# Homes and load times of the weights of three stages, and the lag of the windowed attention, in a two-block transformer kernel on one core

## The chip, the cores and the metric

The kernel runs on one core of a Trainium2 chip. The core has TensorE (PE, matrix products, with its weight loads as PEld), VectorE (DVE), ScalarE (ACT), GpSimd (POOL) and SyncE (SP, which here only issues transfers); each works through its own queue in order and waits on semaphores. The metric is the device time of one execution in microseconds, as the median of several runs.

## The reference

Two transformer blocks over 2048 tokens of width 1024, all in float32. The change touches the first block and the start of the second:

```
proj = rms_norm(x) @ w_in;  q, k, v, z_attn, u_ssm, z_ssm, g = split(proj)
attn   = windowed_gqa(q, k, v, sink, rel_table) * silu(z_attn)   # 8 heads of 64, 2 kv heads
                                                                 # blocks of 128, keys of blocks n-1, n, n+1
ssm    = ...                                                     # recurrent branch, done earlier
merged = sigmoid(g_attn) * (attn @ w_branch_attn) + sigmoid(g_ssm) * (ssm @ w_branch_ssm)
x      = x + merged @ w_out
x      = rms_norm(x) * final_gain                                # end of block one
h      = rms_norm(x) * gain * (1 + scale) + shift                # block two
proj   = h @ w_in_2   # latent q and kv, rope part, x_lru and g_lru of a recurrent branch
```

After that the second block does its recurrent branch (RG-LRU), a latent attention, an output product and a mixture of 32 experts; none of it is changed.

## The kernel before

The program is written engine by engine: `tensor`, `vector`, `scalar`, `gpsimd` and `sync` call the parts of each stage in the order in which that engine runs them. Waits name events (`at("win_ve", "O", j)` is: VectorE has finished output j); a wait for an event with a negative index is none. The on-chip memory is one array, `arena`; `reg(kb, ...)` is a place in it, kb in KB per partition, and stages reuse places by hand. A float32 product of 128 x 128 by 128 x 512 is two TensorE instructions in the trace.

**First attention (`te_win`, `ve_win`, `ac_win`, `po_win`, L1225 to L1394).** 32 jobs (16 query blocks, each in two halves of four heads). A job j has, in order: two pairs of score products (TensorE, L1233), bias and minimum (VectorE, L1248), exp with sum (ScalarE, L1259), reciprocal of the sum (VectorE, L1278), scaling of four heads by it (GpSimd, L1286, four instructions), transposes of the scaled probabilities ("turns", TensorE, L147), their evacuation by ScalarE (L152) or VectorE (L158) in alternation, products with V (TensorE, L1318), and a multiply into `attnT` (VectorE, L1335). Each engine has a loop over steps j in which it works on job j's scores and on the turns and products of job j-2; the third product and the finish belong to job j-3. Probabilities lie in four buffers `Pb`, so the reduction of job j waits for the last turn of job j-4. Jobs 0, 1, 30 and 31 have two key blocks, all others three.

**Branches (`sp_br`, `te_br`, `ve_br`).** Eight blocks d of 128 output channels, each with four tiles u of 512 tokens. A tile is four products with `attnT` into one bank and four with `ssmT` into the next; VectorE multiplies both by gates `sga`, `sgs` (1 MB each a block, loaded by SyncE, double buffered) and adds them into `mgT(d)`. The weights `BW` of a block (0.5 MB) are double buffered at 128 and 132 KB and loaded by SyncE once the whole attention is done (`win_done`) and the block two before is multiplied.

**First output (`sp_out`, `te_out`, `ve_out`, `ac_out`).** 16 row blocks i of 128 tokens, two halves c of 512 channels; a half is eight products (16 instructions). The weights `WO` (2 MB a half) lie at 128 and 144 KB and are loaded once VectorE has the last sum of the branches (`br_done`). VectorE adds x (loaded per row block by SyncE, issued behind the store of the row block before), ScalarE sums squares, VectorE norms (`rsqrt`, a chain of small operations), and norms again to `hn(i)`; TensorE transposes hn(i) in `te_out_turn` two row blocks later.

**Recurrent branch of block two (`te_ll` and others).** It starts with a product with `LX[0]` (`w_lx`, 1 MB a quarter, at 144 and 152 KB), then `te_out_turn` of row block 14, a second product, the turn of row block 15, and the latent product. Its first loads are issued by `sp_ll_first` behind the last products of the output stage.

Of the kernel before, what the change touches and what calls it, by code (L numbers as in the profile page):

```python
# [91 lines left out]
def build(nc, T, out):  # L92
    ctx = ExitStack()
    with ctx:
# [1112 lines left out]
        JOBS = 2 * NT  # L1207
# [114 lines left out]
        def sp_win(s):  # L1322
            for g in range(4):
                for n in range(80, 96):
# [4 lines left out]
                               ).then_inc(*dma(f"ld_z{g % 2}", "za", g))  # L1329

# [13 lines left out]
        def te_win(t):  # L1344
            for j in range(JOBS + 4):
                if win_jobs(j):
                    te_win_score(t, j, 0)
                if win_jobs(j - 3):
                    te_win_pv(t, j - 3, 2)
                if win_jobs(j - 2):  # L1350
                    te_win_turn(t, j - 2, 0)
                    te_win_turn(t, j - 2, 1)
                if win_jobs(j):
                    te_win_score(t, j, 1)
                if win_jobs(j - 2):
                    te_win_pv(t, j - 2, 0)
                    te_win_turn(t, j - 2, 2)
                    te_win_pv(t, j - 2, 1)

        def ve_win(v):  # L1360
            for j in range(JOBS + 4):
# [4 lines left out]
                if win_jobs(j - 2):  # L1366
                    for u in range(2):
                        if (TURN[j - 2] + u) % 2:
                            any_win_turn(v, j - 2, u)
# [3 lines left out]
                if win_jobs(j - 3):  # L1373
                    ve_win_finish(v, j - 3)
                if win_jobs(j - 2) and (TURN[j - 2] + 2) % 2:
                    any_win_turn(v, j - 2, 2)

        def ac_win(a):
            for j in range(JOBS + 4):
                if win_jobs(j):  # L1380
                    ac_win_score(a, j, 0)
                if win_jobs(j - 2):
                    for u in range(2):
                        if (TURN[j - 2] + u) % 2 == 0:
                            any_win_turn(a, j - 2, u)
# [3 lines left out]
                if win_jobs(j - 2) and (TURN[j - 2] + 2) % 2 == 0:  # L1389
                    any_win_turn(a, j - 2, 2)  # L1390
# [16 lines left out]
        BW = [reg(128, 8, 128), reg(132, 8, 128)]  # L1407
# [5 lines left out]
        def sp_br(s):  # L1413
            win_done(s)
            for d in range(8):
                i = d % 2
                s.wait_ge(*at("br_pe", "ssm", d - 2, 3))
                s.do.dma_start(BW[i].rearrange("p a b -> p (a b)"), T["w_br"][d]).then_inc(*dma(f"ld_w{i}", "w_br", d))
# [4 lines left out]
                s.do.dma_start(sgs[i], sgd[8 + d]).then_inc(*dma(f"ld_sgs{i}", "sg", d))  # L1423

# [6 lines left out]

        def te_br(t):
            win_done(t)
            for d in range(8):
                t.wait_ge(*at(f"ld_w{d % 2}", "w_br", d))
# [1690 lines left out]
```

## Time and profile before

| | |
|---|---|
| median of 3 runs | 3802.64 us (3801.28 to 3806.53) |
| the profiled execution | 3799.97 us, span 3798.2 us |
| busy share of the span | PE 93%, PEld 48%, DVE 45%, ACT 27%, POOL 26% |
| first attention | about 1247 to 1431 us |
| branches | about 1435 to 1658 us |
| first output | about 1668 to 1905 us |

Times in the profile count from the start of the span. The views used are: busy time by stretch (with the granted TensorE clock as a share of 2.4 GHz), who waited for whom, the instructions in order of time, and a line's own instructions with its transfers' time from issue to landing. In the order of time, an idle stretch before an instruction stands in brackets with what ended it, and equal neighbours are merged (xN).

### The profile page before, as it was taken

What the parts mean: (1) busy time and instruction counts of PE and PEld (TensorE: products, weight loads), DVE (VectorE), ACT (ScalarE), POOL (GpSimd) and SP (SyncE); (2) the same over time, 40 slices, a digit from 0 to 9 for tenths busy, and PEclk for the clock granted to TensorE, in tenths of its full rate; (3) what the DMA queues carried; (4) which work ended last, traced back from release to release, by engine and by line L of the source; (5) the groups of instructions that cost most, each with busy time, mean ns of one, the idle gap of its engine ahead of it and who ended that gap; (6) DMA issues with size and microseconds to landing.
All of it is one profiled execution on the core that took longest, in us unless ns stands there. A gap on an engine that the chain in (4) does not pass through costs nothing. (4 is left out here: it accounts for less than half of the span.)

```text
span 3798.2 us, 33238 instructions
## 1 busy us (share of the span) xinstructions
PE 3520.1 (93%) x11453; PEld 1840.8 (48%) x11453; DVE 1700.3 (45%) x4081; ACT 1037.5 (27%) x2543; POOL 975.9 (26%) x1362
## 2 busy tenths in 40 slices
PE   4999999999999899989999998999989987999997
PEld 3754455555445444434444445555555553444443
DVE  4656633343354672326665557534444452122121
ACT  3122222211100560002244446433322222222221
POOL 0277777200000680000000005555620001212111
PEclk7999999999999999999999999999999988999999
DMA  3134445434253002221221000001012216999997
GB/s 135 57 126 145 154 142 168 153 100 133 93 177 128 34 12 111 111 78 67 78 91 41 12 11 4 1 1 45 23 47 89 83 72 251 329 329 329 323 325 238
DMA packets 115563, 459.96 MB, mean 121 GB/s; under 512 B 13587, under 2 KB 41107, under 8 KB 103356
## 3 DMA queue, kind: packets, MB, share of 16 engines
q1 hardware_dynamic: 91484, 370.18, 27.4%
q0 software_dynamic: 18432, 67.12, 6.3%
q10 hardware_dynamic: 5472, 20.45, 1.4%
q8 instruction: 94, 1.54, 0.2%
q14 instruction: 81, 0.66, 0.1%
HBM read 340.28 MB, written 117.42 MB: 121 GB/s over the span
## 5 line engine op out<-in xcount | busy, mean ns | idle before, releaser
L142 PE MATMUL pst<-arena 128*128 128x512 f32 (+5 forms) x6938 | 2755.9, 555 | 87.6 <-DVE arena L158 34.0
L142 PEld LDWEIGHTS pst<-arena 128*128 128x128 f32 x6938 | 1301.4, 198 | 1420.5 <-issue 1264.0
L164 POOL TENSOR_TENSOR arena<-arena 128x4 f32<-128x4 f32 (+7 forms) x784 | 401.4, 512 | 463.9 <-DVE arena L2024 403.5
L164 DVE TENSOR_TENSOR arena<-arena 128x1 f32<-128x1 f32 (+8 forms) x1260 | 455.6, 362 | 95.4 <-ACT arena L2254 20.2
L147 PE MATMUL pst<-arena 128*128 128x128 f32 x2145 | 322.4, 289 | 141.6 <-DVE arena L246 52.6
L147 PEld LDWEIGHTS pst<-arena 128*128 128x128 f32 x2145 | 257.1, 147 | 299.8 <-issue 142.9
L1286 POOL TENSOR_SCALAR arena<-arena 128x384 f32<-128x384 f32 (+1 forms) x128 | 151.6, 1202 | 573.0 <-DVE arena L1278 573.0
L153 ACT ACTIVATE arena<-pst,arena 128x128 f32<-128x128 f32 (+1 forms) x630 | 244.0, 482 | 115.1 <-PE pst L147 115.1
L2201 POOL TENSOR_SCALAR arena<-arena 128x512 f32<-128x512 f32 (+3 forms) x160 | 218.3, 1383 | 174.8 <-DVE arena L164 158.6
L167 DVE TENSOR_SCALAR arena<-arena 128x1 f32<-128x1 f32 (+11 forms) x581 | 142.2, 245 | 190.1 <-DMA arena<-in_bc 78.4
L173 ACT ACTIVATE arena<-arena 128x1024 f32<-128x1024 f32 x48 | 50.7, 1057 | 628.0 <-DVE arena L1522 371.6
L2834 POOL DMA_INDIRECT out<-arena x48 | 75.9, 1581 | 492.2 <-DMA out<-arena 338.5
L170 DVE SCALAR_TENSOR_TENSOR arena<-arena,pst 128x256 f32<-128x256 f32 x96 | 43.3, 451 | 355.1 <-ACT arena L2795 353.5
L152 ACT ACTIVATE arena<-pst 128x512 f32<-128x512 f32 (+3 forms) x242 | 120.2, 517 | 253.8 <-PE pst L142 197.6
L170 DVE SCALAR_TENSOR_TENSOR arena<-arena 128x512 f32<-128x512 f32 (+4 forms) x251 | 167.0, 665 | 33.8 <-ACT arena L1735 22.1
L2248 ACT ACTIVATE arena<-pst,arena 128x512 f32<-128x512 f32 (+3 forms) x160 | 98.2, 619 | 225.2 <-DVE arena L2232 225.2
L158 DVE COPY arena<-pst 128x512 f32<-128x512 f32 (+2 forms) x202 | 108.9, 546 | 85.4 <-PE pst L147 37.8
L539 ACT ACTIVATE arena<-pst,arena 128x512 f32<-128x512 f32 x64 | 44.0, 687 | 371.5 <-PE pst L142 371.5
L2308 PE MATMUL pst<-arena 128*128 128x256 f32 (+1 forms) x576 | 142.1, 370 | 0.0
L2232 DVE TENSOR_REDUCE arena<-pst 128x2 f32<-128x1024 f32 (+2 forms) x80 | 85.3, 1066 | 126.8 <-PE pst L2216 125.7
L2795 ACT ACTIVATE arena<-pst 128x256 f32<-128x256 f32 x48 | 18.4, 384 | 442.0 <-PE pst L142 442.0
L2763 POOL DMA_INDIRECT arena<-h2d,arena x48 | 47.5, 989 | 355.6 <-DVE arena L2732 337.4
(194 smaller groups left out, 2102.9 us busy)
## 6 DMA issues: line engine op xcount, KB each, us to landing
arena<-in_w_exp SPq DMA_DIRECT2D x48, 3072.0 KB, 11.9
arena<-in_w_ada SPq DMA_DIRECT2D x48, 512.0 KB, 4.7
rotd<-arena POOLq DMA_DIRECT2D x32, 512.0 KB, 4.3
arena<-rotd SPq DMA_DIRECT2D x32, 512.0 KB, 4.8
arena<-sgd SPq DMA_DIRECT2D x16, 1024.0 KB, 7.5
arena<-pwd SPq DMA_DIRECT2D x32, 416.0 KB, 5.8
pwd<-arena SPq DMA_DIRECT2D x16, 576.0 KB, 5.8
h2d<-arena SPq DMA_DIRECT2D x17, 512.0 KB, 2.9
```

The costliest lines, as they stand in the source:

```text
L142: x = t.do.matmul(o, l, r, start=(i == 0), stop=(i == len(pairs) - 1))
L147: x = t.do.transpose(o, i, ident[0:i.shape[0], 0:i.shape[0]])
L152: return a.do.activation(o, i, ACT.Copy)
L153: return a.do.activation(o, i, ACT.Identity, bias=0.0 if bias is None else bias, scale=1.0 if scale is None else scale)
L158: return v.do.tensor_copy(o, i)
L164: own(v, s).tensor_tensor(o, a, b, op).then_inc(*inc(s, *event))
L167: own(v, s).tensor_scalar(o, a, s1, s2, o1, o2).then_inc(*inc(s, *event))
L170: own(v, s).scalar_tensor_tensor(out=o, in0=a, scalar=sc, in1=b, op0=o1, op1=o2).then_inc(*inc(s, *event))
L1286: p.do.tensor_scalar(P_x, P_x, es[:, c:c + 1], None, MUL).then_inc(*inc("win_po", *(["P", j] if x == 3 else [])))
L2201: p.do.tensor_scalar(P_x, P_x, ff[:, r % 4, x, c:c + 1], None, MUL).then_inc(*inc("mla_po", "P", n, x))
L2248: a.do.activation(ring(n, x)[:, 0:w], bank(2 * (n % 2) + x)[:, 0:w], ACT.Exp, bias=mn[:, r % 4, x, c:c + 1], scale=-1.0, accum_out=ls4[:, ...
L2308: last_ = t.do.matmul(bank(6 + x)[:, w], V2[:, 2 * hp + x, j, :], PT2[n % 4][:, 256 * l:256 * l + 256][:, w], start=(j == 0), stop=(j == 2 ...
```

## The change

Four parts:

1. In the first attention, turns and the first two products belong to job j-3 in step j, the third product and the finish to job j-4. All loops have 37 steps, not 36.
2. The weights of branch blocks 0 and 1 are loaded into new places (48 and 52 KB) during the attention, behind its last load of z; blocks 2 to 7 use 144 and 148 KB. The first two tiles of block 0 stand in TensorE's queue at the head of steps 32 and 33 of the attention, where it has no more scores. A tile waits only for the part of `attnT` that it reads.
3. The first half of w_out stays at 128 KB and is loaded once TensorE has the first product group of block 7; the second half is at 104 KB, where `ssmT` was, and is loaded at `br_done`. TensorE's first four groups go (0,0), (1,0), (0,1), (1,1) as (row block, half). The load of the final gain goes behind that of x.
4. The first two quarters of w_lx are loaded from the third row block of the output stage on, not at its end.

```diff
...
                 s.wait_ge(*at("win_ve", "O", 8 * (g - 1) - 1) if g >= 2 else at("qkv_pe", "tile", 23))
                 s.do.dma_start(Zb[g % 2], zad[:, :, g * 512:(g + 1) * 512].rearrange("m p t -> p m t")
                                ).then_inc(*dma(f"ld_z{g % 2}", "za", g))
+            for d in range(2):
+                s.do.dma_start(BW[d].rearrange("p a b -> p (a b)"), T["w_br"][d]).then_inc(*dma(f"ld_w{d}", "w_br", d))
 
         def ve_win_finish(v, j):
             n, m = j // 2, 2 * (j % 2)
...
             return 0 <= j < JOBS
 
         def te_win(t):
-            for j in range(JOBS + 4):
+            for j in range(JOBS + 5):
                 if win_jobs(j):
                     te_win_score(t, j, 0)
+                elif j < JOBS + 2:
+                    te_br_tile(t, 0, j - JOBS)
+                if win_jobs(j - 4):
+                    te_win_pv(t, j - 4, 2)
                 if win_jobs(j - 3):
-                    te_win_pv(t, j - 3, 2)
-                if win_jobs(j - 2):
-                    te_win_turn(t, j - 2, 0)
-                    te_win_turn(t, j - 2, 1)
+                    te_win_turn(t, j - 3, 0)
+                    te_win_turn(t, j - 3, 1)
                 if win_jobs(j):
                     te_win_score(t, j, 1)
-                if win_jobs(j - 2):
-                    te_win_pv(t, j - 2, 0)
-                    te_win_turn(t, j - 2, 2)
-                    te_win_pv(t, j - 2, 1)
+                if win_jobs(j - 3):
+                    te_win_pv(t, j - 3, 0)
+                    te_win_turn(t, j - 3, 2)
+                    te_win_pv(t, j - 3, 1)
 
         def ve_win(v):
-            for j in range(JOBS + 4):
+            for j in range(JOBS + 5):
...
                 if win_jobs(j - 1):
                     ve_win_sum(v, j - 1)
-                if win_jobs(j - 2):
+                if win_jobs(j - 3):
...
-                if win_jobs(j - 3):
-                    ve_win_finish(v, j - 3)
+                if win_jobs(j - 4):
+                    ve_win_finish(v, j - 4)
...
         def po_win_all(p):
             for j in range(JOBS):
...
         sga = [reg(160, S), reg(176, S)]
         sgs = [reg(168, S), reg(184, S)]
         m1, m2 = reg(152, 512), reg(154, 512)
-        BW = [reg(128, 8, 128), reg(132, 8, 128)]
+        BW = [reg(48, 8, 128), reg(52, 8, 128)] + 3 * [reg(144, 8, 128), reg(148, 8, 128)]
 
         def gate_stored(e, d):
             for n in range(4 * d, 4 * d + 4):
...
             win_done(s)
             for d in range(8):
                 i = d % 2
-                s.wait_ge(*at("br_pe", "ssm", d - 2, 3))
-                s.do.dma_start(BW[i].rearrange("p a b -> p (a b)"), T["w_br"][d]).then_inc(*dma(f"ld_w{i}", "w_br", d))
+                if d >= 2:
+                    if d >= 4:
+                        s.wait_ge(*at("br_pe", "ssm", d - 2, 3))
+                    s.do.dma_start(BW[d].rearrange("p a b -> p (a b)"), T["w_br"][d]
+                                   ).then_inc(*dma(f"ld_w{i}", "w_br", d))
                 s.wait_ge(*at("br_ve", "sum", d - 2, 3))
                 gate_stored(s, d)
                 s.do.dma_start(sga[i], sgd[d]).then_inc(*dma(f"ld_sga{i}", "sg", d))
                 gate_stored(s, 8 + d)
                 s.do.dma_start(sgs[i], sgd[8 + d]).then_inc(*dma(f"ld_sgs{i}", "sg", d))
+            s.wait_ge(*at("br_pe", "attn", 7, 0))
+            s.do.dma_start(WO[0].rearrange("p a b -> p (a b)"), T["w_out"][0]).then_inc(*dma("ld_w0", "w_out", 0))
 
         def br_bank_free(b):
             if b < 4:
...
                 return PT_evac(TURN[JOBS] - 2 + (b - TURN[JOBS]) % 2)
             return at("win_ve", "O", JOBS - 2 + b - 6)
 
+        def te_br_tile(t, d, u):
+            us = slice(u * 512, (u + 1) * 512)
+            t.wait_ge(*at(f"ld_w{d % 2}", "w_br", d))
+            for j in range(8 * u + 6, 8 * u + 8):
+                t.wait_ge(*at("win_ve", "O", j))
+            t.wait_ge(*(at("br_ve", "m1", d - 1, u) if d else br_bank_free(2 * u)))
+            mm(t, bank(2 * u), [(BW[d][:, k, :], attnT[:, k, us]) for k in range(4)]
+               ).then_inc(*inc("br_pe", "attn", d, u))
+            t.wait_ge(*(at("br_ve", "m2", d - 1, u) if d else br_bank_free(2 * u + 1)))
+            mm(t, bank(2 * u + 1), [(BW[d][:, 4 + k, :], ssmT[k][:, us]) for k in range(4)]
+               ).then_inc(*inc("br_pe", "ssm", d, u))
+
         def te_br(t):
-            win_done(t)
             for d in range(8):
-                t.wait_ge(*at(f"ld_w{d % 2}", "w_br", d))
-                for u in range(4):
-                    us = slice(u * 512, (u + 1) * 512)
-                    t.wait_ge(*(at("br_ve", "m1", d - 1, u) if d else br_bank_free(2 * u)))
-                    mm(t, bank(2 * u), [(BW[d % 2][:, k, :], attnT[:, k, us]) for k in range(4)]
-                       ).then_inc(*inc("br_pe", "attn", d, u))
-                    t.wait_ge(*(at("br_ve", "m2", d - 1, u) if d else br_bank_free(2 * u + 1)))
-                    mm(t, bank(2 * u + 1), [(BW[d % 2][:, 4 + k, :], ssmT[k][:, us]) for k in range(4)]
-                       ).then_inc(*inc("br_pe", "ssm", d, u))
+                for u in range(0 if d else 2, 4):
+                    te_br_tile(t, d, u)
 
         def ve_br(v):
             win_done(v)
...
         hn = [reg(180 + 4 * i, 1024) for i in range(2)]
         junk4 = reg(188, 1024)
         ss2, rin2 = cols[:, 144:160], cols[:, 160:176]
-        WO = [reg(128, 8, 512), reg(144, 8, 512)]
+        WO = [reg(128, 8, 512), reg(104, 8, 512)]
 
         def h1_evac(i, hb):
             return at("out_ac" if hb else "out_ve", "h1", i, hb)
 
         def sp_out(s):
             br_done(s)
-            s.do.dma_start(fgb, T["fgb"]).then_inc(*dma("ld_fgb", "fgb"))
-            for c in range(2):
-                s.do.dma_start(WO[c].rearrange("p a b -> p (a b)"), T["w_out"][c]).then_inc(*dma(f"ld_w{c}", "w_out"))
+            s.do.dma_start(WO[1].rearrange("p a b -> p (a b)"), T["w_out"][1]).then_inc(*dma("ld_w1", "w_out", 1))
             for i in range(NT + 1):
                 if i < NT:
                     s.wait_ge(*at("out_ve", "x1", i - 2, 1))
                     s.do.dma_start(xt[i % 2], T["x"][i * 128:(i + 1) * 128, :]).then_inc(*dma(f"ld_xt{i % 2}", "x", i))
+                    if i == 0:
+                        s.do.dma_start(fgb, T["fgb"]).then_inc(*dma("ld_fgb", "fgb"))
+                    if i == 2:
+                        sp_ll_weights(s)
                     if i == NT - 1:
                         sp_ll_first(s)
                     s.wait_ge(*at("out_ve", "x2", i))
...
             br_done(t)
             for i in range(NT):
                 for c in range(2):
-                    b = (2 * i + c) % 4
-                    t.wait_ge(*at(f"ld_w{c}", "w_out"))
-                    t.wait_ge(*at("out_ve", "x1", i - 2, c))
-                    mm(t, bank(b), [(mgT(k)[:, i * 128:(i + 1) * 128], WO[c][:, k, :]) for k in range(8)]
-                       ).then_inc(*inc("out_pe", "x1", i, c))
+                    i_, c_ = (c, i) if i < 2 else (i, c)
+                    t.wait_ge(*at(f"ld_w{c_}", "w_out", c_))
+                    t.wait_ge(*at("out_ve", "x1", i_ - 2, c_))
+                    mm(t, bank((2 * i_ + c_) % 4),
+                       [(mgT(k)[:, i_ * 128:(i_ + 1) * 128], WO[c_][:, k, :]) for k in range(8)]
+                       ).then_inc(*inc("out_pe", "x1", i_, c_))
                 if i >= 2:
                     te_out_turn(t, i - 2)
 
...
             s.do.dma_start(lp[:, :, 0:8], T["lrup"]).then_inc(*dma("ld_lrp", "lrup"))
             for c in range(2):
                 s.wait_ge(*at("out_pe", "x1", NT - 1, c))
-            s.do.dma_start(LX[0].rearrange("p a b -> p (a b)"), T["w_lx"][0]).then_inc(*dma("ld_w0", "w_lx", 0))
             s.do.dma_start(WL.rearrange("p a b -> p (a b)"), T["w_lat"]).then_inc(*dma("ld_lat", "w_lat"))
             s.do.dma_start(pI, T["posb"]).then_inc(*dma("ld_pos", "pos"))
-            s.do.dma_start(LX[1].rearrange("p a b -> p (a b)"), T["w_lx"][1]).then_inc(*dma("ld_w1", "w_lx", 1))
+
+        def sp_ll_weights(s):
+            for i in range(2):
+                s.wait_ge(*at(f"ld_w{i}", "w_out", i))
+                s.do.dma_start(LX[i].rearrange("p a b -> p (a b)"), T["w_lx"][i]).then_inc(*dma(f"ld_w{i}", "w_lx", i))
 
         def sp_ll(s):
             s.wait_ge(*at("out_pe", "h1", NT - 1, 1))
```

`ac_win` changes its indices in the same way.

## Rows read from the trace of the kernel before

**Rows 1.** Busy time by stretch: stretch, us, each engine's busy us, PEclk, DMA, GB/s

```profile
1256.00:1258.00 2.00, 2.00 (x9) 1.55 (x9) 0.51 (x1) 0.60 (x1) 2.00 (x3) 0.50 0.00 0
...
1320.00:1360.00 40.00, 35.89 (x226) 17.34 (x228) 28.93 (x96) 24.86 (x76) 35.30 (x29) 1.00 0.08 27
...
1445.00:1660.00 215.00, 211.80 (x494) 93.48 (x492) 64.81 (x94) 0.00 (x0) 0.00 (x0) 1.00 0.20 74
```

**Rows 2.** Waits of TensorE, 1240 to 1435: total us, times, longest

```profile
PE pst L147 <- POOL arena L1286: 19.9, 17, 3.3
```

**Rows 3.** Order of time, TensorE, steady attention: start, us, what

```profile
1322.47 0.92 PE L1233 MATMUL pst<-arena 64*128 64x384 f32 x4
...
1324.96 1.09 PE L147 MATMUL pst<-arena 128*128 128x128 f32 x8 [0.99 <-POOL arena L1286]
...
1330.13 1.09 PE L147 MATMUL pst<-arena 128*128 128x128 f32 x8
...
1334.60 0.65 PE L1318 MATMUL pst<-arena 128*64 128x256 f32 x4
...
1336.24 1.09 PE L147 MATMUL pst<-arena 128*128 128x128 f32 x8 [0.99 <-POOL arena L1286]
```

**Rows 4.** GpSimd: two jobs in the order of time; its line L1286, ns min/median/max

```profile
1263.63 9.77 POOL L1286 TENSOR_SCALAR arena<-arena 128x384 f32<-128x384 f32 x8 [4.61 <-DVE arena L1278]
...
L1286 POOL TENSOR_SCALAR arena<-arena x128: 912/1242/1247, 1251.8 to 1427.3; 128x384 f32<-128x384 f32 x112, 128x256 f32<-128x256 f32 x16
```

**Rows 5.** Order of time, ScalarE, the last exp of a step in steady attention

```profile
1325.22 0.18 ACT L1259 ACTIVATION_READ_ACCUMULATOR arena<-arena 128x1 f32 x1
```

**Rows 6.** Order of time, GpSimd, its first two jobs

```profile
1251.79 7.24 POOL L1286 TENSOR_SCALAR arena<-arena 128x256 f32<-128x256 f32 x8 [548.23 <-DVE arena L1278]
```

**Rows 7.** Order of time, end of the attention and start of the branches

```profile
1415.17 1.09 PE L147 MATMUL pst<-arena 128*128 128x128 f32 x8 [1.12 <-POOL arena L1286]
...
1424.65 1.09 PE L147 MATMUL pst<-arena 128*128 128x128 f32 x8
1425.35 0.60 ACT L152 ACTIVATE arena<-pst 128x512 f32<-128x512 f32 x1 [1.80 <-PE pst L147]
...
1425.99 1.19 PE L1318 MATMUL pst<-arena 128*64 128x256 f32 x8 [0.25 <-ACT arena L152]
...
1435.16 15.21 PE L142 MATMUL pst<-arena 128*128 128x512 f32 x31 [4.36 <-DMA arena<-in_w_br]
```

**Rows 8.** Line L1423, loads of `sgs` (behind those of `sga`): landing

```profile
DMA to landing us min/median/max: 7.4/8.0/13.3
```

**Rows 9.** VectorE's last sum, TensorE's first products of w_out, landing of L1481

```profile
1657.56 0.69 DVE L164 TENSOR_TENSOR arena<-arena 128x512 f32<-128x512 f32 x1
...
1667.83 42.83 PE L142 MATMUL pst<-arena 128*128 128x512 f32 x96 [11.03 <-DMA arena<-in_w_out]
...
DMA to landing us min/median/max: 9.0/12.1/15.1
```

**Rows 10.** Order of time, VectorE, first two row blocks of the output stage

```profile
1683.22 0.69 DVE L1522 TENSOR_TENSOR arena<-pst,arena 128x512 f32<-128x512 f32 x1 [6.08 <-PE pst L142]
...
1694.30 0.69 DVE L1522 TENSOR_TENSOR arena<-pst,arena 128x512 f32<-128x512 f32 x1 [4.86 <-DMA arena<-in_x]
...
1696.96 0.69 DVE L1522 TENSOR_TENSOR arena<-pst,arena 128x512 f32<-128x512 f32 x1 [1.96 <-PE pst L142]
...
1705.94 0.75 DVE L167 TENSOR_SCALAR arena<-arena 128x1024 f32<-128x1024 f32 x1
```

**Rows 11.** Order of time, TensorE and hn(14) of VectorE, end of the output stage

```profile
1905.59 8.83 PE L142 MATMUL pst<-arena 128*128 128x512 f32 x16 [4.14 <-DMA arena<-in_w_lx]
...
1909.76 0.75 DVE L167 TENSOR_SCALAR arena<-arena 128x1024 f32<-128x1024 f32 x1
...
1922.00 1.04 PE L147 MATMUL pst<-arena 128*128 128x128 f32 x8
...
1931.13 30.29 PE L142 MATMUL pst<-arena 128*128 128x512 f32 x72 [2.08 <-DVE arena L170]
```

More of the change, by code:

```diff
@@ L1365, in ve_win @@
                     ve_win_sum(v, j - 1)
-                if win_jobs(j - 2):
+                if win_jobs(j - 3):
                     for u in range(2):
-                        if (TURN[j - 2] + u) % 2:
-                            any_win_turn(v, j - 2, u)
+                        if (TURN[j - 3] + u) % 2:
+                            any_win_turn(v, j - 3, u)
                 if win_jobs(j):
@@ L1372, in ve_win @@
                     ve_win_sink(v, j)
-                if win_jobs(j - 3):
-                    ve_win_finish(v, j - 3)
-                if win_jobs(j - 2) and (TURN[j - 2] + 2) % 2:
-                    any_win_turn(v, j - 2, 2)
+                if win_jobs(j - 4):
+                    ve_win_finish(v, j - 4)
+                if win_jobs(j - 3) and (TURN[j - 3] + 2) % 2:
+                    any_win_turn(v, j - 3, 2)
         def ac_win(a):
-            for j in range(JOBS + 4):
+            for j in range(JOBS + 5):
                 if win_jobs(j):
                     ac_win_score(a, j, 0)
-                if win_jobs(j - 2):
+                if win_jobs(j - 3):
                     for u in range(2):
-                        if (TURN[j - 2] + u) % 2 == 0:
-                            any_win_turn(a, j - 2, u)
+                        if (TURN[j - 3] + u) % 2 == 0:
+                            any_win_turn(a, j - 3, u)
                 if win_jobs(j):
@@ L1388, in ac_win @@
                     ac_win_sink(a, j)
-                if win_jobs(j - 2) and (TURN[j - 2] + 2) % 2 == 0:
-                    any_win_turn(a, j - 2, 2)
+                if win_jobs(j - 3) and (TURN[j - 3] + 2) % 2 == 0:
+                    any_win_turn(a, j - 3, 2)
         def po_win_all(p):
```

## The prediction

> **What bounds the kernel now.** I read the stages that the diff touches, in three steps. First the table by stretch: between 1320 and 1360 us (first attention) TensorE is busy 35.9 of 40 us, in the branches (1445 on) 211.8 us for 494 instructions, that is 0.429 us each and no hole until 1656.8 [rows 1]. So in these stages TensorE's own queue sets the end, and a hole in it costs its full length. Then who made the holes: in the first attention and its run-in, GpSimd's scaling of the probabilities ended 19.9 us of TensorE's waits, 17 of them, the longest 3.3 [rows 2]. Last the joints between the stages, where it waits for weights: 4.36 us for w_br [rows 7], 11.03 us for w_out [rows 9], 4.14 us for w_lx [rows 11]. The change is aimed at these four places. Everything later keeps its order and only starts earlier.
>
> **1. Three steps of lag in the steady attention.** One job now goes from turns to turns in 5.17 us (1324.96 to 1330.13), the next in 6.11 (to 1336.24), 11.28 a pair, and the wait stands in the second: its last product starts at 1334.60 and lasts 0.58, so the job was through at 1335.18 and waited 1.06 [rows 3]. GpSimd isn't full: two jobs in a row take it 9.77 us, 4.885 a job [rows 4], against 5.64 on average. It starts late, since its reciprocal comes from VectorE one step later; a third step gives its result 5 us more. Then the floor is TensorE. The job that waits for nothing takes 5.05 (1330.13 to 1335.18). For its neighbour, whose first turn is evacuated by ScalarE, the wait has so far hidden something: ScalarE's exps of that step end at 1325.40, 2.9 us after the score's start at 1322.47; a copy and its signal take 0.64 (1425.35 to 1425.99), so the first product can't start before 3.5 to 3.55, where TensorE would be there after 3.30 [rows 3, 5, 7]. I take 0.2 for it: 5.25, and 10.3 a pair, 5.15 a job. Bounds: 5.05 (no new wait) and 5.64 (nothing won).
>
> Four probability buffers remain. Job j's score reduction waits for the last turn of job j-4, which TensorE now issues one step earlier, ahead of the score itself; so no new wait of VectorE, and nothing is queued behind one. The three queues are re-ordered alike, no instruction is added.
>
> **The run-in.** GpSimd starts at 1251.79, does two jobs with two keys in 7.24, to 1259.03, then 4.885 each [rows 4, 6]. So job 3 is ready at 1268.80, and TensorE, held at job 2 until 1263.97, turns it at about 1269.1. From there 5.15 a job, less 0.6 for shorter scores at the end: turns of job 28 at 1269.1 + 25 x 5.15 - 0.6 = 1397.2, now 1415.17 [rows 7]. Gain 18.0. The 3.3 us hole before the first turns (at 1255.5), after which the clock stood at 0.50 [rows 1, 2], gets 1.7 us of scores and splits into pieces; if the clock falls all the same, job 3 is turned 1.5 later (low end of the gain).
>
> **2. First two branch tiles inside the run-out.** A tile is 8 products of two instructions, 16 x 0.429 = 6.86 us [rows 1]. From the turns of job 28: rest of that step 3.4, tile 6.86, job 29 3.7, tile 6.86, third product of 29 0.6, job 30 2.53, job 31 2.53 (1424.65 to 1427.18 now), 26.5 in all: the attention ends at 1423.7 with two tiles done. GpSimd's last job is through some 6.5 us after the last score, covered by the first tile; the turns of jobs 29 and 30 stand behind the tiles in TensorE's queue, and with them only work of this same run-out. Today the first tile starts at 1435.16 after a hole of 4.36, and its first instructions run slow: 31 take 15.21 us, not 13.3 [rows 7]. Its weights are loaded from about 1351 on, in the middle of the attention, 80 us ahead, so their price is nothing. Thirty tiles remain, 205.8 us: the branches end at 1629.5 against 1656.8. **Gain of parts 1 and 2: 27.3 us.**
>
> The cover for the gates: SyncE still issues them only after the last output of the attention, and VectorE needs both for the first tile. The second of the two landed after 7.4 to 13.3 us [rows 8]; TensorE now has two tiles, 13.7 us, before it wants the first bank back, and 17.2 before the second. With the median (8.0) that leaves some 8 us; with the longest (13.3, plus 0.7 for the multiply) it still holds. Cost 0, upper bound 2. The wait for landed w_br stands in TensorE's queue at the first tile, long met. Weights of block 2 are issued behind the gates of block 1 and needed 41 us later. Moving weights behind the gate loads at d = 3 costs nothing for the same reason.
>
> **3. w_out.** The first half now has a home that no branch weight uses and is issued when TensorE begins block 7, some 25 us ahead; both halves need 15.1 us today [rows 9]. So TensorE waits only for VectorE's last sum, which ends at 1658.25, 1.45 after the branches' last product [rows 1, 9]: a hole of 1.5 in place of 11.03. The slow start goes too: 96 instructions took 42.83, not 41.2 [rows 9]; the hole of 2.08 in [rows 11] was followed by none. The second half is issued at the sum, as the first transfer, 2 MB. The first half, with 0.5 MB ahead, landed 9.0 us after its issue [rows 9]; TensorE wants the second at 13.7 thanks to the order (0,0), (1,0), (0,1), (1,1). Covered by 4 us.
>
> But that order has a price. Row block 0 is complete at S+20.6 (S the start of the stage) where it was at +13.7, and VectorE's chain hangs on it: from the add of (0,1) to the add of (1,0), through norm, store and the load of x that SyncE issues only behind them, 11.08 us (1683.22 to 1694.30); from (1,1) to the end of hn(0) 9.7 (1696.96 to 1706.69) [rows 10]. So hn(0) ends at 20.7 + 11.1 + 0.7 + 9.7 = S+42.2, and TensorE wants it at S+41.2. A new wait of 1.0 us, once. Branch end to turn(0) is 1.5 + 42.2 = 43.7, now 1710.5 - 1656.8 = 53.7 (its 96 instructions, 42.8 less the overlap of their modelled end, behind 1667.83) [rows 9]. **Gain 10.0 us.** SyncE's new wait (first product of block 7) has only the w_out load and the next stage behind it. The two loads of w_lx now go out behind the third x, done 10 us before SyncE's next.
>
> **4. w_lx.** Gone are the 4.14 us and the slow first instructions (16 in 8.83, not 6.9) [rows 11], 6.0 together. What is late next is hn(14), which VectorE ends at 1910.51; TensorE would be there 6.86 after 1901.4, at 1908.3, so 2.2 comes back, and from turn(15) to the first gates (9.13 us, 1922.00 to 1931.13, with the existing wait of 2.08) nothing moves [rows 11]. Turn(15) then comes at 1910.6 + 0.9 + 6.9 = 1918.4, 3.6 earlier than 1922.0. **Gain 3.6 us.** Bounds 2 and 6.
>
> **Sum:** 27.3 + 10.0 + 3.6 = 40.9 us. The profiled execution took 3799.97 (span 3798.2), so 3759.1; the median of the runs stands 2.7 above it: 3802.64 - 40.9 = **3761.7 us**.
>
> **Clock.** The rows show the low level (0.50, 1.2 GHz) after holes of 3.3 us and more, full clock behind the one of 2.08 [rows 11], and full clock through the 1 us holes of the attention [rows 1 to 3]. All holes I expect are below 2.5.
>
> **A rule against lag.** The row first: GpSimd's instructions on three keys have a median of 1242 and a maximum of 1247 ns, though VectorE's sum and difference of each job fall into them [rows 4]. The Trainium skill (SBUF — State Buffer, section "SBUF: two separate sides") says that GpSimd and VectorE share one port pair under an exclusive lock, and that a VectorE operation with two SBUF inputs blocks GpSimd for its whole length. By it GpSimd, with 95% of the new step taken, would be stretched. The trace shows no stretching.
>
> **Rivals.**
> - **GpSimd becomes the bound** (0.06). If two or three small VectorE operations a job (0.17 us each) held it, a job would last 5.4: 25 x 0.25 = 6 us less, **3768**. For: 4.885 leaves only 0.26. Against: the maximum of 1247 ns. It is the lock rule's result.
> - **The lag wins nothing** (0.06), because another loop (ScalarE's exps, evacuation, product) holds the job near 5.6: 25 x 0.45 = 11 less, **3773**. Against: the free job of 5.05.
> - **New joint waits or low clock** (0.12): gates at their longest landing 2, low clock at run-in 1.5 and after the 1.5 us hole 1.5, third joint only 2: 5 to 7 less, **3767**.
> - **A bit more** (0.13): 5.05 a job and full 6 at w_lx: 5 more, **3757**.
> - **Slower than before** (0.02): the four-buffer ring. If VectorE's reduction of job j had to follow the last turns of j-4 in series, each step would be 5.15 + 1.2 (two reductions) + 0.6 (exp) = 6.95, 1.3 over today's for 32 steps, +42, against 9 + 10 + 3.6 from the run-out and the joints: **3822**. It decides from 6.35 a job on. Against: that turn stands before the score in TensorE's own queue.
> - **The change doesn't do what it says** (0.01): loads still late because SyncE is stuck in an earlier wait, **3775**. Its waits there are all for things long past.
> - My forecast, 3761.7 within 3: 0.60.
>
> **How the numbers follow.** 3755 to 3772 takes in the forecast, the better case, the joint case and the lock; it leaves out the useless lag, the ring and the last, 0.09, and what I have missed, some 0.1. About 0.2% (8 us) is what a measurement can tell; all cases but the ring and something unforeseen lie further below than that: faster 0.95, same 0.02, slower 0.03.
>
> **What would show it.** Right: turns every 5.1 to 5.3 us without waits for GpSimd after job 3; no wait for w_br, w_out or w_lx; the attention with two tiles over near 1424; holes of 1.5 before the first product of w_out, 1 before turn(0), 2.3 before turn(14). Wrong: waits of TensorE's products for ScalarE's copies over 0.3 each; GpSimd instructions beyond 1250 ns; clock below 1 behind a 1.5 us hole; the first multiply of the branches later than 13 us after the last attention output.

## The result, and the profile after

| | before | after |
|---|---|---|
| median | 3801.96 us (3799.89 to 3806.53, 4 runs) | 3764.33 us (3749.46 to 3767.74, 4 runs) |
| ratio after to before | | 0.9885, 95% interval 0.9857 to 0.9912 |
| the profiled execution | 3799.97 us, span 3798.2 | 3749.46 us, span 3747.6 |

The median moved 37.6 us, the profiled execution 50.5. When two numbers for one change differ like this, the first thing to do is to cut both spans at the same two events: TensorE's first score product of the attention, and the first gate products of the recurrent branch of block two (at 1931.13 before [rows 11]). Busy time by stretch of the kernel before, cut there (stretch, its length, busy us of the five engines, PEclk, DMA share, GB/s):

```profile
0.00:1247.74 1247.74, 1168.79 (x3418) 632.62 (x3419) 588.71 (x1046) 247.09 (x429) 412.74 (x843) 0.98 0.39 130
1247.74:1931.13 683.39, 638.61 (x2192) 296.72 (x2193) 351.29 (x1144) 170.50 (x465) 151.96 (x129) 0.98 0.22 79
1931.13:3798.20 1867.07, 1712.69 (x5843) 911.50 (x5843) 760.29 (x1892) 619.92 (x1649) 411.22 (x390) 0.96 0.38 130
```

and of the kernel after:

```profile
0.00:1234.14 1234.14, 1166.17 (x3418) 632.07 (x3419) 581.55 (x1046) 247.25 (x429) 424.14 (x843) 0.98 0.40 132
1234.14:1880.43 646.29, 632.79 (x2192) 294.46 (x2193) 351.28 (x1144) 168.89 (x465) 151.99 (x129) 1.00 0.23 84
1880.43:3747.60 1867.17, 1714.65 (x5843) 911.87 (x5843) 759.84 (x1892) 620.92 (x1649) 412.22 (x390) 0.96 0.38 130
```

The changed stages took 37.1 us less (683.39 to 646.29), and TensorE was idle 44.8 us in them before (683.39 less 638.61), 13.5 after; the other 5.8 us of the gain are busy time, products that no longer run at the lower clock (PEclk 0.98 and 1.00). The last stretch is the same to 0.1. The other 13.6 us lie ahead of the first score, where the code is unchanged; they are no gain of the change (more on this below). From here on every time of a stage is counted from the first score, which makes executions comparable to a few tenths as far as the joints. There the slow starts (the first products behind a long hole, run at the lower clock) differ between executions of one kernel: two executions of the kernel before differ by 3.2 us at the first gates, three of the kernel after by 2.0.

**Attention.** TensorE in the order of time, after, three turns in a row, then GpSimd over four jobs, its line L1286 (ns min/median/max), and all that TensorE waited for between 1240 and 1435:

```profile
1318.54 1.09 PE L147 MATMUL pst<-arena 128*128 128x128 f32 x8
...
1323.59 1.09 PE L147 MATMUL pst<-arena 128*128 128x128 f32 x8
...
1328.80 1.09 PE L147 MATMUL pst<-arena 128*128 128x128 f32 x8
```

```profile
1309.55 9.96 POOL L1286 TENSOR_SCALAR arena<-arena 128x384 f32<-128x384 f32 x8 [0.31 <-DVE arena L1278]
1319.81 9.96 POOL L1286 TENSOR_SCALAR arena<-arena 128x384 f32<-128x384 f32 x8 [0.30 <-DVE arena L1278]
```

```profile
L1286 POOL TENSOR_SCALAR arena<-arena x128: 914/1248/1278, 1238.2 to 1392.3; 128x384 f32<-128x384 f32 x112, 128x256 f32<-128x256 f32 x16
```

```profile
PE pst L1318 <- ACT arena L152: 2.4, 5, 0.7
PE pst L147 <- POOL arena L1286: 0.8, 1, 0.8
PE pst L1233 <- DVE arena L1248: 0.4, 1, 0.4
PE pst L1318 <- DVE arena L158: 0.3, 1, 0.3
```

Steps of 5.05 and 5.21 in place of 5.17 and 6.11 [rows 3], and one wait for GpSimd, 0.8, in place of 17 with 19.9 [rows 2]. A row of eight of GpSimd's instructions is two jobs with the short pause between them counted in, so its busy time is read from the view by stretch, 18 jobs before and 12 after (the fifth engine is GpSimd):

```profile
1286.18:1387.67 101.49, 92.14 (x578) 44.44 (x580) 73.80 (x244) 62.76 (x190) 88.22 (x73) 1.00 0.06 22
```

```profile
1309.55:1371.14 61.59, 61.01 (x386) 29.64 (x386) 48.88 (x163) 41.15 (x127) 58.93 (x49) 1.00 0.10 35
```

GpSimd works 4.90 us a job before and 4.91 after, now in a step of 5.13: it is nearly full (58.93 of 61.59) and no slower. Single instructions last up to 1278 ns, 1247 before [rows 4].

**Run-out and start of the branches**, TensorE:

```profile
1388.14 7.13 PE L142 MATMUL pst<-arena 128*128 128x512 f32 x16
...
1398.98 7.13 PE L142 MATMUL pst<-arena 128*128 128x512 f32 x16
...
1409.09 1.09 PE L147 MATMUL pst<-arena 128*128 128x128 f32 x8
1410.43 1.19 PE L1318 MATMUL pst<-arena 128*64 128x256 f32 x8 [0.25 <-ACT arena L152]
1411.55 38.89 PE L142 MATMUL pst<-arena 128*128 128x512 f32 x90
```

The two tiles stand between the last jobs, the third tile follows the last attention product with no hole, and 90 instructions run in 38.89 us, full clock from the first one (31 took 15.21 in [rows 7]). VectorE's first two multiplies wait for their gates, and nobody waits for them:

```profile
1416.97 0.69 DVE L164 TENSOR_TENSOR arena<-pst,arena 128x512 f32<-128x512 f32 x1 [4.88 <-DMA arena<-sgd]
1419.43 0.69 DVE L1468 TENSOR_TENSOR arena<-pst,arena 128x512 f32<-128x512 f32 x1 [1.77 <-DMA arena<-sgd]
```

**The later joints**, TensorE: first products of w_out, turn(0), turn(14), the second product of w_lx, first gates (turn(i) is the transpose of hn(i)), then the stretch behind turn(14)'s start:

```profile
1619.32 41.47 PE L142 MATMUL pst<-arena 128*128 128x512 f32 x96 [1.51 <-DVE arena L164]
1661.70 1.09 PE L147 MATMUL pst<-arena 128*128 128x128 f32 x8 [0.91 <-DVE arena L167]
...
1861.82 1.93 PE L147 MATMUL pst<-arena 128*128 128x128 f32 x8 [2.24 <-DVE arena L167]
1863.54 7.92 PE L142 MATMUL pst<-arena 128*128 128x512 f32 x16
...
1880.43 30.28 PE L142 MATMUL pst<-arena 128*128 128x512 f32 x72 [2.08 <-DVE arena L170]
```

```profile
1861.82:1865.20 3.38, 3.38 (x10) 2.40 (x11) 2.02 (x9) 1.41 (x4) 0.00 (x0) 0.51 0.13 50
```

1.51 in place of 11.03 [rows 9], the new wait of 0.91 for hn(0), and 2.24 for hn(14) in place of 4.14 for w_lx [rows 11]. One thing is new: the turn behind the 2.24 us hole took 1.93, not 1.09, and the product after it 7.92, not 7.03. The clock fell: 0.51 was granted in these 3.4 us.

### The profile page after: what moved, and what is told of

Same layout as the page of the kernel before. It is cut to its first block and busy times, and to the rows that moved or that the text cites. A ratio compares the mean times of both kernels' runs of the same rounds, so it can differ in the third digit from the quotient of the medians.

```text
span 3747.6 us, 33237 instructions
## 1 busy us (share of the span) xinstructions
PE 3513.6 (94%) x11453; PEld 1838.4 (49%) x11453; DVE 1692.7 (45%) x4081; ACT 1037.1 (28%) x2543; POOL 988.4 (26%) x1362
## 5 line engine op out<-in xcount | busy, mean ns | idle before, releaser
L164 POOL TENSOR_TENSOR arena<-arena 128x4 f32<-128x4 f32 (+7 forms) x784 | 412.7, 526 | 465.3 <-DVE arena L2043 404.9
L164 DVE TENSOR_TENSOR arena<-arena 128x1 f32<-128x1 f32 (+8 forms) x1260 | 445.4, 354 | 95.3 <-ACT arena L2273 20.2
L1286 POOL TENSOR_SCALAR arena<-arena 128x384 f32<-128x384 f32 (+1 forms) x128 | 151.7, 1213 | 523.8 <-DVE arena L1278 522.6
```

What stands on the lines that cost most here:

```text
L164: own(v, s).tensor_tensor(o, a, b, op).then_inc(*inc(s, *event))
L1286: p.do.tensor_scalar(P_x, P_x, es[:, c:c + 1], None, MUL).then_inc(*inc("win_po", *(["P", j] if x == 3 else [])))
```

## The experiments

All numbers in us from the first score, each from one profiled execution: the first turns of job 28, the end of the branches, the turns of row blocks 0 and 13 in the output stage, and the first gate products of block two. The branches end 1.51 ahead of the first product of w_out (in kernels that wait for weights there, by that hole). How sure one number is can be seen from kernels that are alike up to it: seven executions with the attention and branches of after end the branches at 383.6 to 383.7, the two of before at 409.1 and 409.6.

| kernel | turns job 28 | branches end | turn(0) | turn(13) | first gates |
|---|---|---|---|---|---|
| before | 167.4 | 409.1 | 462.8 | 652.7 | 683.4 |
| before_again | 167.6 | 409.6 | 464.9 | 654.8 | 686.6 |
| lag_alone | 150.5 | 391.4 | 445.2 | 635.1 | 666.6 |
| weights_alone | 167.7 | 403.3 | 447.2 | 637.2 | 666.0 |
| lag_undone | 167.6 | 401.6 | 445.1 | 635.1 | 662.2 |
| tiles_late_b | 150.5 | 384.1 | 427.6 | 617.6 | 644.7 |
| order_undone | 150.6 | 383.7 | 427.7 | 617.7 | 644.7 |
| wout_late | 150.6 | 383.7 | 437.7 | 627.7 | 654.7 |
| lx_late | 150.6 | 383.7 | 427.3 | 617.3 | 648.7 |
| after | 150.6 | 383.7 | 427.6 | 617.5 | 646.3 |
| after_again | 150.6 | 383.7 | 427.3 | 617.2 | 644.3 |
| after_third | 150.6 | 383.7 | 427.7 | 617.6 | 644.7 |
| joints | 150.5 | 383.6 | 426.5 | 616.4 | 641.5 |

**1. lag_alone**: the kernel before with the lag and nothing else.

```diff
...
                 if win_jobs(j - 3):
-                    te_win_pv(t, j - 3, 2)
-                if win_jobs(j - 2):
-                    te_win_turn(t, j - 2, 0)
-                    te_win_turn(t, j - 2, 1)
+                    te_win_turn(t, j - 3, 0)
+                    te_win_turn(t, j - 3, 1)
...
```

> The kernel before with three steps of lag and nothing else. My theory (GpSimd's result came one step late, TensorE is the floor): turns 5.05 and 5.21 us apart as in the kernel after, turns of job 28 at 150.6 us from the first score (167.4 before), the last product of the branches at 389 us from the first score (409.1 before), since the run-out no longer waits for GpSimd but still stands before late weights; 20 us less in all, about 3782. Rival, that GpSimd's rate or the port pair it shares is the bound: 5.4 or more a job, 8 us less at most. Rival, that the gain came from the run-in with its low clock: steps stay 5.17 and 6.11, 5 us less.

Measured: steps of 5.05 and 5.22, turns of job 28 at 150.5, as in after. Both rivals fall: the steps changed, so it was not the run-in alone, though that gave part of it (job 3 is turned at 22.4 in place of 26.0, 3.6 of the 16.9 us at job 28). Ratio to before 0.9969 (0.9946 to 0.9991), medians 3788.01 and 3807.08. Branches end at 391.4, not 389. About half of the miss is that the attention ends 18.9 us earlier, not 20; the other half is that the joint behind grew by 1.2:

```profile
1410.55 1.18 PE L1318 MATMUL pst<-arena 128*64 128x256 f32 x8 [0.25 <-ACT arena L152]
1416.30 8.92 PE L142 MATMUL pst<-arena 128*128 128x512 f32 x14 [4.57 <-DMA arena<-in_w_br]
```

The wait for weights is 4.57 here, 4.36 in [rows 7], and 14 instructions take 8.92 where 6.3 is full speed (14 x 0.429, and 0.27 more for the modelled end of a row's last product): a slow start of 2.6, against 1.6 in [rows 7], where 31 take 15.21 and full speed is 13.6. Work that is saved ahead of such a joint does not shorten it. Gain of the lag alone at the branches' end: 17.7.

**2. lag_undone**: after with two steps of lag.

> The kernel after with two steps of lag again; early weights, the two branch tiles in the run-out and the later loads stay. My theory: steps 5.17 and 6.11 as before, turns of job 29 at 172.3 us from the first score, and then the tiles hide GpSimd's last two jobs, so the branches end at 401 us from the first score (383.7 in the kernel after), 17 to 18 us more than after, though the lag alone gives 20: the two parts share the last 2 us. If they did not overlap it would be 403.5. About 3782.

Measured: branches end at 401.6, 17.9 more than after, ratio 0.9942 (0.9917 to 0.9967). The place was right (401), the overlap was not: the lag is worth 17.9 on top of the rest and 17.7 alone, so the parts seem to add up. Two effects of some 1.2 us cancel: the tiles are worth 1.7 at two steps of lag (the turns of the last two jobs stand behind tiles here with no wait) and 0.4 at three, and lag_alone paid 1.2 more at its joint. With neither in play, from weights_alone to tiles_late_b below, the lag is worth 19.2.

**3. tiles_late_b**: after with the first two tiles behind the attention.

```diff
-                elif j < JOBS + 2:
-                    te_br_tile(t, 0, j - JOBS)
...
-                for u in range(0 if d else 2, 4):
+                for u in range(4):
```

(and SyncE waits for the first product of blocks 0 and 1 before it loads blocks 2 and 3.)

> The kernel after with the first two tiles of the branches back at the head of the branch stage; weights still loaded early, with a wait of SyncE before it loads those of blocks 2 and 3. Theory A, mine: once the weights lie ready and the lag hides GpSimd, the run-out has no hole worth a tile; TensorE waits only some 0.5 us for the last output and the clock does not fall: branches end at 383 to 384 us from the first score, as in the kernel after (383.7). Theory B: the tiles are what covers the last jobs and the gate loads; without them TensorE waits some 5 us and starts slow, branches end at 389 or later.

```profile
1408.71 1.19 PE L1318 MATMUL pst<-arena 128*64 128x256 f32 x8 [0.25 <-ACT arena L152]
1409.83 20.44 PE L142 MATMUL pst<-arena 128*128 128x512 f32 x47
```

TensorE's first tile follows the last product at once, with no hole and no slow start; the tile needs only the outputs of the first eight jobs. Branches end at 384.1, 0.4 later than in after. Theory A holds, and the hole is even smaller than the 0.5 I gave it. Whole time: ratio 0.9927 (0.9900 to 0.9954), medians 3768.98 and 3807.08, six runs from 3756.8 to 3781.3: far too coarse for a difference of 0.4.

**4. weights_alone**: the same with two steps of lag as well.

> The kernel after with two steps of lag and the first two branch tiles behind the attention: of the first two parts of the change only the early weights are left. Mine: the attention ends as before, 183.5 us from the first score, TensorE waits only for the last output, some 0.5 us, and nothing starts slow; branches end at 403.5 us from the first score (409.1 before, 401.6 with the tiles at the same lag, 383.7 in after). So tiles are worth 2 us where GpSimd is waited for and 0.4 where not. Rival, that a wait for gates stands behind: 405 or more.

```profile
1429.33 1.09 PE L147 MATMUL pst<-arena 128*128 128x128 f32 x8 [1.09 <-POOL arena L1286]
...
1431.79 18.72 PE L142 MATMUL pst<-arena 128*128 128x512 f32 x43
```

Branches end at 403.3 (403.5 expected). Against lag_undone the tiles are worth 1.7, about what TensorE waits in this run-out (1.09 for GpSimd's last job, shown, and 0.54 for a copy of VectorE), and with three steps of lag 0.4. The early weights are worth 409.1 - 403.3 = 5.8: hole and slow start.

**5. order_undone**: the kernel after with the first four groups of w_out in plain order.

```diff
-                    i_, c_ = (c, i) if i < 2 else (i, c)
+                    i_, c_ = i, c
```

> The kernel after with the first four groups of the output product in plain order (0,0), (0,1), (1,0), (1,1). Mine: the second half of w_out lands 7.5 to 8 us after the stage's start, TensorE wants it at 6.9, a hole of about 1 there; the hole of 0.9 before the first turn goes, since row block 0 is complete 6 us earlier; first turn at 42.0 us from the stage's start, 42.4 in the kernel after: no difference. Rival, that the order is what hides the load: hole of 3 us or more and a slow start, first turn at 45 or later.

```profile
1627.25 7.13 PE L142 MATMUL pst<-arena 128*128 128x512 f32 x16 [1.51 <-DVE arena L164]
1635.34 34.60 PE L142 MATMUL pst<-arena 128*128 128x512 f32 x80 [0.96 <-DMA arena<-in_w_out]
1669.78 1.04 PE L147 MATMUL pst<-arena 128*128 128x128 f32 x8
```

The hole is 0.96 at the second group and none at turn(0), which comes 42.5 after the stage's start (42.0 expected, 42.4 in after). The order trades one hole of a microsecond for another. It decides nothing here.

**6. wout_late**: after with both halves of w_out loaded at the branches' end.

> The kernel after with both halves of w_out loaded at the end of the branches. Mine: the first half lands some 7.6 us after its issue, so a hole of 9.2 us and a slow start of 1.5; the second half is hidden by the order of the groups; from the last branch product to turn(0) 53 us, not 43.9: 9 more. Rival, that the new order of the groups alone recovers most of it: 48 or less.

```profile
1639.35 43.87 PE L142 MATMUL pst<-arena 128*128 128x512 f32 x96 [9.49 <-DMA arena<-in_w_out]
1683.88 1.09 PE L147 MATMUL pst<-arena 128*128 128x128 f32 x8 [0.66 <-DVE arena L167]
```

A hole of 9.49 and 2.4 of slow start (43.87 against 41.47 in after); from the branches' end to turn(0) 54.0 us, 43.9 in after. The early load is worth 10.1.

**7. lx_late**: after with the loads of w_lx behind the last output product.

```diff
-                    if i == 2:
-                        sp_ll_weights(s)
...
+            sp_ll_weights(s)
             s.do.dma_start(WL.rearrange("p a b -> p (a b)"), T["w_lat"]).then_inc(*dma("ld_lat", "w_lat"))
```

> The kernel after with the first two loads of w_lx issued behind the last output products, as before. Mine: TensorE waits 4.1 us for them and starts slow, the hole ahead of turn(14) goes, and from turn(13) to the first gates 30.7 us pass instead of 27.0. Rival, that a chain through VectorE sets this joint: 28 or less.

```profile
1872.95 9.59 PE L142 MATMUL pst<-arena 128*128 128x512 f32 x16 [4.13 <-DMA arena<-in_w_lx]
1882.38 1.04 PE L147 MATMUL pst<-arena 128*128 128x128 f32 x8
```

From turn(13) to the first gates 31.5 us (30.7 expected). The hole of 4.13 comes back, the one ahead of turn(14) goes, as expected; the start is slower than in [rows 11] (9.59 for 16 instructions, 8.83 there). The early load is worth 4.4 against after_again.

**8. after_again and after_third**: the kernel after twice more.

> The kernel after once more, for its spread and the clock behind the hole of 2.24 us ahead of turn(14). Mine: within the changed stages nothing moves (branches end 383.7 us from the first score, turn(0) 42.4 after the output stage's start); the whole time moves by some 10 us between executions with a stage ahead of the change (its first score lies anywhere from 1232 to 1248 us); the clock behind that hole stays at full speed this time as in three other kernels with the same hole, and from turn(13) to the first gates 27.0 us pass, not 28.8. Rival: the clock falls there every time in this kernel.

> The kernel after once more beside it. Mine: 39 us less than before in the changed stages (first gates 644.3 us from the first score, or 646 where the clock falls behind the hole of 2.24 us), and 39 give or take 6 in the whole time, the rest of the 48 that the last comparison showed being chance. Rival, that the change also shortens the stretches around it: 45 or more again.

Behind the same hole as in after, the clock stayed up (after_again):

```profile
1875.54 1.09 PE L147 MATMUL pst<-arena 128*128 128x128 f32 x8 [2.24 <-DVE arena L167]
1876.47 7.03 PE L142 MATMUL pst<-arena 128*128 128x512 f32 x16
```

and turn(13) to first gates took 27.1 in both, not 28.8. Whole times: 3763.60 against 3811.31, ratio 0.9873 (0.9854 to 0.9893), and 3769.99 against 3806.24, ratio 0.9901 (0.9878 to 0.9924). The first ratio stands for 48 us, the second for 38, which is what the stages say; and their intervals overlap; so nothing shows that the extra 10 of the first belong to the change.

**9. before_again**: the kernel before against itself.

> The kernel before, unchanged, against itself: what a comparison of whole times can tell here. Mine: a ratio within 0.3% of 1, stages of the change as known (branches end 409.1 us from the first score, first gates 683.4); the stretches ahead of the first score and behind the first gates differ by up to 15 us between executions. Rival, that this execution's stretches ahead and behind are the same as in the first profile (1247.7 and 1867.1).

Ratio 1.0000 (0.9986 to 1.0015), with single runs from 3794.18 to 3810.74. I had expected the stages to come as before; they are 3.2 us longer than in the first profile (686.6): the joints again, with a hole of 5.03 for w_br and slower starts at w_out and w_lx. The stretch ahead took 1250.4, the one behind 1868.4. Counted against this execution, the change is worth 42.3 and 41.9 us in the two repeats of after, not 39.1 and 38.7.

**10. joints**: after with x of the second row block loaded at the stage's start, both first products of w_lx ahead of turns 14 and 15, and hn(15) ahead of the evacuation of turn 14.

```diff
...
                 if n < LJ:
                     te_ll_project(t, n, 0)
-                if n == 0:
-                    te_out_turn(t, NT - 2)
...
                 if n < LJ:
                     te_ll_project(t, n, 1)
                 if n == 0:
+                    te_out_turn(t, NT - 2)
                     te_out_turn(t, NT - 1)
...
```

> The kernel after with three edits at the joints: SyncE loads x for the second row block at the stage's start, not behind the first store; TensorE does both products of the first w_lx block ahead of turns 14 and 15; VectorE forms hn(15) before it evacuates turn 14. Mine: the hole ahead of turn(0) goes (first turn 41.2 us from the stage's start, 42.4 in after), the one ahead of turn(14) goes, turn(13) to the first gates takes 25.5 us, not 27.0, since a wait of some 3 us for the first convolution stays; 2 to 3 us less than after in these stages, too little to tell in the whole time. Rival: the chain behind turn(15) only moves, so gates come no earlier than with 27.0.

```profile
1863.57 1.91 PE L147 MATMUL pst<-arena 128*128 128x128 f32 x16
1865.72 6.25 PE L142 MATMUL pst<-arena 128*128 128x448 f32 x16 [0.24 <-DVE arena L161]
1874.10 31.98 PE L142 MATMUL pst<-arena 128*128 128x512 f32 x72 [2.12 <-DVE arena L170]
```

Turn(0) 41.3 after the stage's start with no hole, turn(13) to gates 25.1 (25.5 expected): 2.8 less than after_again at the gates. But here the clock fell behind the hole of 2.12 at the gates (72 instructions in 31.98, 30.28 in after), which gave 1.7 back. Median 3757.62 (5 runs), ratio to before 0.9861 (0.9842 to 0.9881); beside after_again's 0.9873 on the same chip the whole time can't tell it apart.

## Why the prediction was right, point by point

The forecast was 3761.7, measured 3764.3, within the range. In the stages 40.9 us were forecast and 37.1 measured in the profiled execution, 39.1 and 38.7 in the two repeats against the same before, 42.3 and 41.9 against before_again: the forecast lies inside what two executions of either kernel leave open.

- **Lag.** 5.15 a job forecast, (5.05 + 5.21)/2 = 5.13 measured. The mechanism (a result one step late, TensorE the floor) stands by lag_alone. Turns of job 28 came at 150.6 where the sum says 149.5. The miss is in the run-in: job 3 is turned at 22.4, not at 21.4, since three products ahead of it wait 0.56 to 0.68 each for ScalarE's copies, which stand behind its exps; one of them:

```profile
1248.87 1.08 PE L1318 MATMUL pst<-arena 128*64 128x256 f32 x8 [0.68 <-ACT arena L152]
```

  I had charged that wait to the steady step only, where it costs 0.16. The clock, at 0.50 in the run-in of before [rows 1], stayed at 1.00 in that of after, whose longest hole is 0.79; the 1.5 us that I held ready for a fall were not needed.
- **The lock rule.** I wrote that the trace shows no stretching and gave the rival 0.06. Single instructions of GpSimd did pass 1250 ns, which I had set as a sign against me: up to 1278 in after, 1284 in after_again. But in lag_alone and joints, with the same steps, medians are 1242 and 1241 and maxima 1263 and 1258, and a job takes 4.90 in before and lag_alone (58.82 for 12) and 4.91 in after. So the shorter step brought no stretching that costs anything, and the longer instructions differ by execution. The Trainium skill (SBUF — State Buffer, "SBUF: two separate sides") names VectorE's operations with two SBUF inputs as what holds the port; no run here takes them out, so what they cost GpSimd is not shown. GpSimd stays 0.2 under TensorE's step, and it would be the bound next.
- **Tiles in the run-out.** 26.5 forecast for the run-out with two tiles, 26.85 measured (1384.70 to 1411.55; a tile between other products takes 7.07, not 6.86); the rest of the branches 206.3, not 205.8. Together with the run-in: 25.4 for parts 1 and 2, not 27.3. Undone one after the other, the parts are the lag 19.2 (weights_alone less tiles_late_b), the early weights 5.8 (before less weights_alone) and the tiles 0.4 (tiles_late_b less after). So what failed in the reasoning is the credit: once the weights lie ready and the lag hides GpSimd, the run-out has nothing left for the tiles to cover.
- **Slow starts.** The sum read them 0.27 too long each, as it compared a row, whose last product carries a modelled end, with 0.429 an instruction: 1.6 at the branches, not 1.9, 1.4 at w_out (42.83 less 41.47), not 1.6. They are also no constant of the joint: before_again has 1.4, 2.9 and 2.8 at the three joints.
- **Gates.** VectorE had them some 5 and 7 us after the last output, and they cost TensorE nothing, as said.
- **w_out.** 43.7 forecast from the branches' end to turn(0), 43.9 measured; hole 1.5 and 1.51; wait for hn(0) 1.0 and 0.91. wout_late gives the early load 10.1. The second half landed 7.9 us after its issue, wanted at 13.7; but the order that bought this slack won nothing (order_undone), since its price of 0.9 at hn(0) is what it saves.
- **w_lx.** 3.6 forecast, 2.0 measured in the profiled execution, 3.6 in the repeats (30.7 less 27.1). The term was right and the clock was the miss: I had taken all holes below 2.5 us as harmless, from one of 2.08 with full clock behind it.
- **Whole time.** That it came so near the median has luck in it: the four runs of after spread by 18 us on their own, and in the profiled one all three terms fell short, by 1.9, 0.2 and 1.6 us.

Open: what makes the stretch ahead of the attention 1232 to 1252 us long. The profiles show where. TensorE's holes there, before:

```profile
376.89 3.52 PE L628 MATMUL pst<-arena 128*16 128x128 f32 x16 [5.31 <-DVE arena L164]
...
453.03 0.69 PE L147 MATMUL pst<-arena 128*128 128x128 f32 x2 [6.71 <-DMA arena<-pwd]
```

and after:

```profile
441.19 0.41 PE L147 MATMUL pst<-arena 128*128 128x128 f32 x2 [1.76 <-DVE arena L164]
```

The executions with the short stretch (after, lag_undone, joints: 1232 to 1234 us) have only the small hole, the others both large ones or their like (order_undone, in between at 1242, only the second), after_again and after_third with the same code as after among them. So it isn't the change. Why VectorE's work at the first hole and the transfer at the second are late in one execution and not in the next was not tried.

## What to carry to other kernels

Cost the joints between stages before the loops: weights that are loaded when a stage begins cost their landing and a slow start, 5.8, 10 and 2 to 4.4 us here. A home that is free earlier removes that, down to whatever is late next: nothing at the branches, 1.5 us at w_out, 2.2 at w_lx. A lag of one more step cost nothing here, since the four buffers allowed it, and it pays the difference between the waited-for engine's late result and the floor of the busiest one, which must be looked up in a step that did not wait. When executions spread by about as much as the parts of a change are worth, cut the spans at the same two events and compare the stages; and test a change's parts apart, since what is made most of (tiles in the run-out, order of groups) may bring nothing.

## What the runs showed of the hardware that I had not expected

- TensorE's clock can fall to its lower level (0.5, 1.2 GHz) behind a hole of 2.1 to 2.3 us, and mostly doesn't. Behind the hole of 2.24 to 2.26 ahead of turn(14) it fell in two of eight executions (after, weights_alone: from turn(14) to turn(15) 9.5 us, 7.8 in the others), behind the one of 2.08 to 2.12 ahead of the first gates in one of 13 (joints). Each fall cost 1.7 us. The hole of 1.51 ahead of w_out was followed by full clock in all nine executions that have it. That is no safe length: ahead of the attention 0.50 was granted behind holes of 1.70, 1.76 and 1.99 us, each followed by one short group of transposes and a second wait (joints, after, lag_undone).
- The slow start behind a long hole is not one number: 31 instructions took 15.2 us behind a hole of 4.36, 14 took 8.9 behind 4.57, that is 1.6 and 2.6 us over full speed; behind the holes of 11.03 and 11.08 ahead of w_out it was 1.4 and 2.9 (42.83 and 44.36 for 96 instructions, 41.47 at full clock).
- GpSimd's scaling took 4.90 us a job when TensorE's steps were 5.64 apart (88.22 for 18 jobs) and 4.91 when they were 5.13 apart (58.93 for 12), with VectorE's small operations running beside it in both. Single instructions reached 1247 ns in one and 1278 in the other, and 1263 in lag_alone at the same steps.
